# Asking for ScalarE's function tables ahead, one table set for logarithm and exponential, and constant products on TensorE in five pauses

## The reference, cut to what matters

```python
# layer 0
p = rms_norm(x, norm1) @ w_in
y_a = rwkv7_mixer(p[..., :RW_IN], ...)        # tanh, sigmoid, exp of decays; per-head norm of y
y_b = gqa_axial_attention(p[..., RW_IN:], ...) # rms_norm of q and k, rotary, softmax
x = x + concat([y_a, y_b]) @ w_out
x = x + swiglu(rms_norm(x, norm2), gate, up, down)      # silu
# layer 1
p = rms_norm(x, norm1) @ w_in
x = x + gla_mixer(p, ...) @ w_out   # log_sigmoid gates, exp of their sums, rms_norm per head, silu
x = x + moe_swiglu(rms_norm(x, norm2), router, ...)     # top 2 of 8 experts, silu
```

## Time and profile before

| what | value |
|---|---|
| time, median of 3 runs | 1715.87 us (1714.54 to 1717.29) |
| profiled execution, its own time | 1710.24 us |
| its span, first to last instruction | 1708.4 us |
| mean granted clock of TensorE | 0.977 of full speed |
| busy: PE, PEld | 1588.1 us (93%), 1443.0 us (84%) |
| busy: DVE, ACT | 1281.1 us (75%), 1061.5 us (62%) |
| ACT_TABLE_LOADs on ACT | 27, of 1283 ns each |

### The profile page before, as it was taken

One profiled execution on the slowest core, in us unless ns is written; L12 is line 12 of the kernel. 1 busy time (PEld: TensorE's weight loads), 2 busy tenths in 40 slices (PEclk: granted clock), 3 DMA queues, 4 the chain that ended last, 5 costly groups with the idle time before them and its releaser, 6 DMA issues.

```text
span 1708.4 us, 35972 instructions
## 1 busy us (share of the span) xinstructions
PE 1588.1 (93%) x13830; PEld 1443.0 (84%) x13830; DVE 1281.1 (75%) x1750; ACT 1061.5 (62%) x1635; POOL 0.2 (0%) x4
## 2 busy tenths in 40 slices
PE   6987886999989968999999999999999999999996
PEld 6866876999978857898898899898898998998995
DVE  6855336655554765888998988988988988898885
ACT  5653344444444533777777777777776776777773
POOL 0000000000000000000000000000000000000000
PEclk9989998999999989999999999999999999999998
DMA  8002003444443313899899899898998998998992
GB/s 335 1 1 113 4 3 148 160 180 181 184 146 148 112 38 124 295 367 352 327 368 353 329 364 353 328 370 334 341 368 331 347 371 329 347 362 332 348 370 96
DMA packets 71957, 425.37 MB, mean 249 GB/s; under 512 B 8128, under 2 KB 8128, under 8 KB 37712
## 3 DMA queue, kind: packets, MB, share of 16 engines
q1 hardware_dynamic: 71888, 424.38, 66.5%
HBM read 423.30 MB, written 1.05 MB: 248 GB/s over the span
## 4 chain that ended last, share of the span: by engine, by line
PE 57%; DVE 3%; issue 2%; ACT 1%; DVEq 0%; ACTq 0%
PE bank L156 18%; PE bank L157 18%; PE bank L158 17%; PE bank L1704 2%; DVE scratch L1887 1%; PE bank L1728 1%; DVE w_low L153 1%; PE bank L1747 1%; ACT w_high L150 0%; DVE y_low L153 0%; PE bank L1957 0%; DVE scratch L2025 0%; PE bank L1953 0%; DVE scratch L1893 0%; PE bank L1696 0%
## 5 line engine op out<-in xcount | busy, mean ns | idle before, releaser
L153 DVE TENSOR_TENSOR w_low<-ring,w_high 128x1024 fp32r<-128x1024 f32 x801 | 951.1, 1219 | 153.6 <-ACT w_high L150 153.6
L150 ACT ACTIVATE w_high<-ring 128x1024 fp32r<-128x1024 f32 x801 | 810.7, 1052 | 75.1 <-PE bank L158 57.8
L156 PE MATMUL bank<-w_high,slots_high 128*96 128x256 f32 x1792 | 514.8, 287 | 1.2 <-DVE slots_low L153 1.2
L158 PE MATMUL bank<-w_high,slots_low 128*96 128x256 f32 x1792 | 500.7, 279 | 0.0
L157 PE MATMUL bank<-w_low,slots_high 128*96 128x256 f32 x1792 | 500.6, 279 | 0.0
L156 PEld LDWEIGHTS bank<-w_high,slots_high 128*96 128x96 f32 x1792 | 291.0, 162 | 18.0 <-issue 2.2
L157 PEld LDWEIGHTS bank<-w_low,slots_high 128*96 128x96 f32 x1792 | 289.4, 161 | 14.8
L158 PEld LDWEIGHTS bank<-w_high,slots_low 128*96 128x96 f32 x1792 | 290.1, 162 | 0.0
L156 PE MATMUL bank<-x_high,w_high 128*128 128x256 f32 x768 | 225.7, 294 | 33.1 <-PEq L1067 11.5
L157 PE MATMUL bank<-x_low,w_high 128*128 128x256 f32 x768 | 222.1, 289 | 0.0
L158 PE MATMUL bank<-x_high,w_low 128*128 128x256 f32 x768 | 221.6, 289 | 0.0
(11 more groups left out here) (320 smaller groups left out, 1620.8 us busy)
## 6 DMA issues: line engine op xcount, KB each, us to landing
ring<-in_w_moe SPq DMA_DIRECT2D x224, 1024.0 KB, 7.2
ring<-in_w_moe SPq DMA_DIRECT2D x224, 512.0 KB, 7.3
ring<-in_w_ffn SPq DMA_DIRECT2D x22, 1536.0 KB, 6.3
ring<-in_w_in SPq DMA_DIRECT2D x15, 1536.0 KB, 6.6
ring<-in_w_out SPq DMA_DIRECT2D x6, 1536.0 KB, 7.7
scratch<-in_x SPq DMA_DIRECT2D x2, 512.0 KB, 4.1
out_y<-scratch SPq DMA_DIRECT2D x2, 512.0 KB, 3.9
const<-in_const SPq DMA_DIRECT2D x1, 948.0 KB, 13.5
```

Of the source, the lines that this page charges most:

```text
L150: return nc.scalar.activation(dst, src, ACT.Copy)
L153: return nc.vector.tensor_tensor(dst, src, high.bitcast(f32), sub)
L156: nc.tensor.matmul(out, left[0], right[0], start=start, stop=False, **flags)
L158: return nc.tensor.matmul(out, left[1], right[0], start=False, stop=stop, **flags)
```

## The change

Further, a function `keep_running` on PE makes products of two constants (the identity and 256 columns of the constants) into a PSUM bank that holds nothing needed; it is called in five places at which PE waits next: 18 products behind mixer A's variance sums, 5 before and 16 after the turning of the second mixer's outputs, 6 and 6 in the router. Nothing reads what they write.

```diff
+        LOG_EXP, SIGMOIDS, SILU = "natural_log_exp_and_others", "sigmoid_and_others", "silu_and_others"
+        LOG = "natural_log"
...
+        def keep_running(pe, n, bank):
+
+            for _ in range(n):
+                nc.tensor.matmul(ps[bank][:, 0:S], ident, const[:, 0:S], start=True, stop=True)
...
                 sq3 = sq_qk.rearrange("p (a b) -> p a b", a=5)
+                act.preload_act_table_set(LOG_EXP)
                 act.wait_ge(consts_loaded, 32)
                 split_high(act, 0)
                 norm_rstd(act, 0)
                 x_high(act, xn, ready=xn_pair(act, 0))
                 split_high(act, 1)
+                act.preload_act_table_set(SIGMOIDS)
                 take_moving(0)
...
                 nc.scalar.activation(sq3[:, 2:4], two(PAIR_OF[3]), ACT.Square).then_inc(qk_sq_ready, 1)
+                act.preload_act_table_set(LOG_EXP)
                 split_high(act, 4, TILES_DONE[2])
...
                 def key_norm():
+                    act.preload_act_table_set(LOG)
                     act.wait_ge(kk_floor_ready, 1)
                     act_then(act, nc.scalar.activation(flat(kk_scale), flat(kk_scale), ACT.Ln, scale=KK_SCALE))
+                    act.preload_act_table_set(LOG_EXP)
                     nc.scalar.activation(flat(kk_scale), flat(kk_scale), ACT.Exp, scale=-0.5, bias=par("kk_bias")).then_inc(kk_scale_ready, 1)
...
                     nc.tensor.matmul(ps[2 + n][:, :], cst("headsum"), halves(y_sq, n), start=True, stop=True).then_inc(var_ready, 1)
+                keep_running(pe, 18, 4)
...
                 x_high(act, xn, ready=xn_pair(act, 1))
+                act.preload_act_table_set(SILU)
                 act.wait_ge(back_split, G_FFN)
...
             def _(act):
+                act.preload_act_table_set(LOG_EXP)
                 split_high(act, G_IN1)
                 norm_rstd(act, 2)
...
                         nc.scalar.activation(factor, factor, ACT.Exp, scale=GS).then_inc(scales1_ready, 1)
+                        act.preload_act_table_set(SILU)
...
             def _(act):
+                act.preload_act_table_set(LOG_EXP)
                 for n in range(4):
                     act.wait_ge(k1_turned, n + 1)
...
                 state_terms(2)
+                keep_running(pe, 5, 4)
                 for t in range(TT):
...
                             last.then_inc(o_turned, 1)
+                keep_running(pe, 16, 0)
...
                 last.then_inc(logits_ready, 1)
+                keep_running(pe, 6, 7)
                 pe.wait_ge(chosen_ready, 1)
...
+                keep_running(pe, 6, 7)
                 pe.wait_ge(tokens_ready, TT)
                 all_passes(pe, moe_products)
...
                     front_high_part(act, G_MOE + 1, n, 0)
+                act.preload_act_table_set(SILU)
                 all_passes(act, moe_activations)
```

## The result

| | before | after |
|---|---|---|
| time, median of 5 runs each | 1717.20 us (1714.54 to 1718.73) | 1705.63 us (1703.41 to 1707.38) |
| ratio after to before | | 0.9931, 95% interval 0.9917 to 0.9945 |
| profiled execution, own time / span | 1710.24 / 1708.4 us | 1704.87 / 1703.0 us |
| mean granted clock in it | 0.977 | 0.981 |

The ratio is worth 11.8 us of 1717.2 (9.4 to 14.3). Forecast were 1704.0 and 11.9 off. Note already that the two profiled executions lie only 5.4 us of span apart; where the other six went is the most useful part of this case.

A forecast was written before the change was run, and what follows sets the result against it. PE's products, busy 93% of the span, were taken as the bound; 9.8 us from loads plus 2.1 from clock gave 11.9 off, so 1698.3 us profiled and 1704.0 us as median, range 1699 to 1711.

The forecast's parts named there:

- sum of 9.8: Eight places where DVE waits for ACT: table loads that go shorten these waits, together by 9.8 us.
- Third norm and gates: One load saved at each: 0.8 us at the third norm, 1.28 us at the logarithm of the gates.
- Gain 0 at the norm of the keys: Norm of the keys: two loads stay, the first with no idle time in front to hide it; gain 0.
- The constant products: Five calls in PE's pauses: 0.45 us a call of two instructions, clock gain 2.1 us at the second output projection.
- the pause of 3.70 at 1.00: A PE pause of 3.70 us with full clock throughout, taken as sign that a rest of 1.6 keeps the clock.
- the rival with the clock up at both projections: Rival, 13%: full clock at the first output projection too, 1.6 us more gained, 1702.4 us.
- gain 1.28: First Silu of the experts: one load goes out of DVE's wait of 6.29 us; gain 1.28 us.
- the products cost nothing: All pauses, router included: constant products fit or disappear in PE's 1.17 us wait, at full clock; cost 0.
- Loads only: Rival, 22%: idle rests still pull the clock down at both output projections; only 9.8 us saved, 1706.1 us.
- Half of it lost: Rival, 8%: where PE is bound by products, earlier starts meet weights not yet split; 6 us saved, 1710 us.
- Products that outlast their pauses: Rival, 6%: constant products run at half clock, 0.43 us an instruction, 14 us late against 9.8 saved; 1720 us.
- That the change does nothing: Rival, 6%: the build still puts loads before `Ln` and `Exp`, or the joint set lacks something; 1716 us.

The follow-up runs named there:

- e1_loads: The changed kernel without its five calls of constant products, so the requests for table sets alone: 1705.37 us, ratio 0.9947 to the kernel before.
- a_after: The changed kernel again, no edit, on the chip of three later runs: 1705.03 us, ratio 0.9938 to the kernel before.
- e3: The changed kernel without the two calls of 6 constant products in the router: 1702.48 us, ratio 0.9937 to the kernel before.
- e4: The changed kernel with 25 in place of 18 constant products behind mixer A's variance sums: 1702.73 us, ratio 0.9929 to the kernel before.
- e6: The changed kernel with the keys' norm taken from the joint table set, so both its loads go: 1701.86 us, ratio 0.9923 to the kernel before.
- e7: The changed kernel with 40 in place of 18 constant products at mixer A's head norm: 1710.29 us, ratio 0.9971 to the kernel before.
- e10: The changed kernel with three more calls of constant products (5, 9, 12) in and behind the attention: 1706.38 us, ratio 0.9938 to the kernel before.
- e2_products: The kernel before with the five calls of constant products and no request for a table set: 1714.31 us, ratio 0.9993 to the kernel before.

## Why the prediction was right, point by point

**The loads.** The sum of 9.8 came from one wait at a time, and e1_loads measured 9.1. Place by place the traces agree at the second norm (1.28 in wait and stage), the roots of the second mixer (2.56 in both), the norm of q and k (1.24 in the stage; DVE's wait fell by 1.61, more than the 1.28 forecast), the head norm (0.25, forecast 0.17) and the first norm, whose wait is gone. The first stage gave 1.81, but its length ranges from 19.45 to 21.46 us over the traces of kernels that share its code (after, a_after, e1, e3, e4, e6, e7, e10), and before's 21.29 lies among them; so the stage's length confirms nothing. DVE's wait there is gone in the traces in which the norm's sum takes 3.72 us as in before, and 0.94 to 1.59 us in those of the changed code in which half clock stretches the sum to 5.1 us and more (e3, e4, e7, e10). Third norm and gates were forecast at 0.8 and 1.28; their waits are covered by the clock in the profiled pair and appear in e4_y25, 1.85 for the two, where DVE's wait at the third norm is gone as forecast.

**Gain 0 at the norm of the keys.** Right for this change, which keeps both loads. The words behind it, that nothing hides them, were right too, and the prediction did not follow them to the end: e6_joint shows them worth 2.6.

**The constant products.** 0.22 to 0.24 us an instruction, forecast 0.23; none late. The second output projection gave 1.98, forecast 2.1; the rest ahead of it was 2.27 where 1.6 was forecast, and the clock held all the same, in all twelve traces with the sixteen products (rests of 1.70 to 2.28). The row on which the forecast leaned, the pause of 3.70 at 1.00, was lucky: in eight of ten traces the clock falls there. In the trace of before it falls too behind a pause of 4.69 ahead of the feed-forward loop (0.50 in its first 4 us), which the prediction did not read. The first was counted as 0 because its rest of 3.2 was too near to the one example of 3.70; the rest was 3.49, and the clock fell 2.1 us into the pause's idle part, by the windows. That choice was right, and the rival with the clock up at both projections falls: in all six traces with a rest of 3.49 to 3.75 us there, the first 5 us of the projection were granted 0.50 to 0.70, and in the six with a longer call, which leaves 0.6, they were granted 1.00.

**The step that failed** is "gain 1.28" at the experts' first Silu, together with "the products cost nothing" in the router. The prediction saw that the gather would run faster and that DVE would not let PE go on sooner, and stopped there. It didn't ask what a longer wait does to the clock, though it used that very argument at the projections in the same paragraph. PE's wait of 1.17 us became 2.91, 14 instructions fewer went through in the next 4.05 us, and in each trace of the changed kernel the load saved at the Silu was given back. The words "it already ends before DVE lets PE go on" were true of the trace of before by a hair: in four of the six traces without the router's products DVE waits 0.4 to 1.5 us for the gather. So the products also protect against something that the prediction didn't see, and taking them out isn't a gain that the times show. The term is some 1.3 us, too small to be seen in the time, so the forecast stood in spite of it.

**The rivals.** Loads only (1706.1): the products' own share is 1.2 us with an interval from -1.0 to 3.3, and changed kernel and e1_loads, 11.8 and 9.1 off, have intervals that overlap, so this rival is not excluded by the times; the trace excludes its reason at the second projection, where the clock held. Half of it lost: the stages whose waits shrank came out shorter by what the waits lost, to within 0.4 us, apart from the first norm's, whose length varies by more than that, the third norm's, where the clock covers it in the profiled pair, and the router's. Products that outlast their pauses: not here, and not at half clock (0.22 to 0.24 us an instruction); that lateness on PE costs its length, as this rival counted it, is what e7_late shows. That the change does nothing: excluded by ten loads in place of 27 and by the interval of the ratio.

**The two medians and the two profiles.** The forecast in the terms of the profiled execution, 1698.3, was 6.6 us too low (1704.87), while the forecast of the median was 1.6 off. Of the 6.6, 2.85 are in a stretch with the same work on every engine at 0.02 less clock, 2.1 at the third norm, 0.9 at the first output projection, 1.28 in the router, less 0.6 at the start. Only the router's part has a cause in the change that the runs show. The 2.85 are a draw: e2_products, which has the code of before up to the head sums, takes 173.53 us in that stretch beside before's 169.72, and the six traces that have the changed kernel's code there (after, a_after, e1, e3, e4, e7) take 169.62 to 172.57. At the first output projection the kernels whose clock fell there take 24.45 to 25.54. The 17 runs of before beside e1 to e4 take 1709.52 to 1719.68 us; the profiled one, 1710.24 with a mean clock of 0.977, was at the quick end of both.

That 11.9 forecast and 11.8 measured lie so close is luck: the interval is 9.4 to 14.3, the same kernel came out at 10.6 in a second set of runs, and the loads and the products measured one by one give 9.1 and 1.2. Without the Silu's 1.28 the prediction's sum would have been 10.6. What the runs confirm is the mechanism, waits of DVE that shrink load by load and the clock at the second output projection, and a saving of some 10 to 12 us.

## What to carry to other kernels

A table load is worth what the engine behind it waits, load by load, and no more: add up the waits and not the loads (27 loads are 34.6 us here, 17 that went are 21.8, and 9 came back). When constant products fill a pause, ask what ends the *next* pause: if another engine decides it, the faster stretch in between makes that pause longer, and the clock can fall there instead (0.58 to 0.63 behind 2.91 us in all seven traces here). And compare medians of many executions with each other, not two profiled executions; a difference of a few us between two profiles can be the clock alone, which windows with equal counts and unequal clock show.

## What the runs showed of the hardware, unexpected

- A pause of one length does not decide the clock: PE waits 3.66 us ahead of the third norm's sum in every kernel that leaves that place unfilled, and the first 4 us of the sum were granted 1.00 in two traces (before, e4_y25) and 0.50 to 0.63 in eight.
- Executions of one and the same kernel on one chip differ by up to 10 us in 1714 (17 runs of before, 1709.52 to 1719.68), with mean clocks of 0.970 to 0.977.
- The mean granted clock is no measure of the gain: products alone raised it from about 0.973 to 0.980 and brought 1.2 us (-1.0 to 3.3).
- No drain beside a table load: with two of them gone a wait of 7.82 us fell by 2.56, twice 1.28.
